# Weight sums by adding transfers for the first two quads, in a Strassen-Winograd decoder layer

## The reference

```python
x = layer_norm(ALPHA * x + merged @ w_out, ln1_g, ln1_b)
f = (jax.nn.silu(x @ w_ff_gate) * (x @ w_ff_up)) @ w_ff_down   # 1024 -> 2816 -> 1024
x = layer_norm(ALPHA * x + f, ln2_g, ln2_b)
```

## Time and profile before

| | |
|---|---|
| time, median of 3 runs | 923.67 us (923.64 to 924.33) |
| the profiled execution | 923.97 us, of which 922.0 us are the span from its first to its last instruction |
| busy, share of the span | PE 99%, weight loads 98%, DVE 83%, ACT 49%, POOL 35% |
| granted clock | 0.998 of full speed |
| moved by DMA | 98.49 MB, mean 107 GB/s |

### The profile page before, as it was taken

The page is one execution under the profiler, slowest core; times in us unless marked ns, Lnnn a source line. Parts: engine busy times, 40 slices in busy tenths (PEclk is TensorE's granted clock), DMA queues, the critical chain, the costliest instruction groups (busy, mean ns, idle before and its releaser), DMA issues.

```text
span 922.0 us, 18574 instructions
## 1 busy us (share of the span) xinstructions
PE 909.7 (99%) x7157; PEld 903.4 (98%) x7157; DVE 768.3 (83%) x1138; ACT 452.3 (49%) x783; POOL 326.5 (35%) x326
## 2 busy tenths in 40 slices
PE   9999999999999999999999999999999999999996
PEld 9999999999999999999999999999999999999995
DVE  3799999999869889877886699998878888878558
ACT  4422232325766634555553466676545666445442
POOL 4666565758300000000005451454732555421102
PEclk9999999999999999999999999999999999999999
DMA  7733332222436524342244221433333433333232
GB/s 228 197 91 92 90 101 85 75 69 79 133 111 230 198 77 125 100 125 81 75 130 124 82 64 29 124 107 93 92 106 95 118 96 92 92 108 92 85 85 97
DMA packets 169525, 98.49 MB, mean 107 GB/s; under 512 B 5306, under 2 KB 165602, under 8 KB 169457
## 3 DMA queue, kind: packets, MB, share of 16 engines
q1 hardware_dynamic: 167225, 96.66, 36.3%
q10 hardware_dynamic: 2232, 0.92, 0.4%
HBM read 89.94 MB, written 7.62 MB: 106 GB/s over the span
## 4 chain that ended last, share of the span: by engine, by line
PE 89%; DVE 6%; ACT 2%; issue 1%; POOL 1%; POOLq 0%; DVEq 0%; ACTq 0%
PE main L1582 38%; PE main L1743 33%; PE aux L1743 5%; PE main L1815 3%; PE aux L1582 3%; PE main L1996 1%; PE aux L1996 1%; PE aux L1568 1%; POOL h_f L914 1%; PE main L1618 1%; DVE aux L2606 0%; ACT merged L1305 0%; DVE merged L2619 0%; PE main L1606 0%; DVE r_tok L2896 0%
## 5 line engine op out<-in xcount | busy, mean ns | idle before, releaser
L785 POOL TENSOR_TENSOR w_lo<-raw,w_hi 128x1024 fp32r<-128x1024 f32 (+1 forms) x46 | 109.9, 2395 | 344.2 <-ACT w_hi L976 336.8
L1582 PE MATMUL main<-x_hi,w_lo 128*128 128x272 f32 x752 | 155.8, 288 | 0.0
L1582 PE MATMUL main<-x_hi,w_hi 128*128 128x272 f32 x752 | 155.6, 288 | 0.0
L1582 PE MATMUL main<-x_lo,w_hi 128*128 128x272 f32 x752 | 155.1, 288 | 0.0
L976 ACT ACTIVATE w_hi<-raw 128x1024 fp32r<-128x1024 f32 x103 | 108.5, 1057 | 70.0 <-PE main L1582 37.6
L1582 PEld LDWEIGHTS main<-x_hi,w_lo 128*128 128x128 f32 x752 | 118.2, 188 | 0.0
L1582 PEld LDWEIGHTS main<-x_lo,w_hi 128*128 128x128 f32 x752 | 118.1, 188 | 0.0
L1582 PEld LDWEIGHTS main<-x_hi,w_hi 128*128 128x128 f32 x752 | 117.4, 189 | 0.0
L2214 DVE SCALAR_TENSOR_TENSOR aux<-glu_pad,miscT,aux 128x512 f32<-128x512 f32 x112 | 75.1, 748 | 0.0
L922 POOL TENSOR_TENSOR h_lo<-h_f,h_hi 128x272 fp32r<-128x272 f32 x50 | 50.4, 1016 | 55.4 <-ACT h_hi L1410 54.6
L1582 PE MATMUL main<-y,w_hi 128*128 128x272 f32 x384 | 63.6, 287 | 0.0
(11 more groups left out here) (464 smaller groups left out, 2919.9 us busy)
## 6 DMA issues: line engine op xcount, KB each, us to landing
raw<-in_w_in SPq DMA_DIRECT2D x63, 512.0 KB, 4.2
raw<-in_w_ff_gate SPq DMA_DIRECT2D x22, 512.0 KB, 4.0
raw<-in_w_ff_up SPq DMA_DIRECT2D x22, 512.0 KB, 5.2
raw<-in_w_branch SPq DMA_DIRECT2D x32, 256.0 KB, 4.0
raw<-in_w_ff_down SPq DMA_DIRECT2D x32, 256.0 KB, 4.0
raw<-in_w_out SPq DMA_DIRECT2D x8, 512.0 KB, 4.2
raw<-in_w_ff_down SPq DMA_DIRECT2D x16, 192.0 KB, 4.3
kept_sums<-g_made_hi SPq DMA_DIRECT2D x4, 544.0 KB, 3.7
```

Of the source, the lines that this page charges most:

```text
L785: pool.tensor_tensor(w_lo[s][:, 0:n, :], raw[s][:, 0:n, :], w_hi[s][:, 0:n, :].bitcast(F32), ALU.subtract).then_inc(w_lo_ready, 1)
L1582: mm = pe.matmul(ps[:, h, :], w[s][:, k, :], x[:, h * HALF:(h + 1) * HALF], start=(first and k == 0 and j == 0), stop=(last and k == n - 1 ...
```

## The change

For steps 0 and 1 the four weight sums are no longer made by DVE. SP loads b11, b22 and b21 a second time, into `w_sum[s][0]`, `[1]` and `[2]` (256 KB each), and POOL issues four transfers that add to what is there: b12 onto the first (T1), T1 onto the second (T2), b22 onto b12 in place (T3), T2 onto the third (T4). The third of these waits with the second for the first, and the fourth waits for both. The signs change with that: all four weight sums are made with plus signs, and the sums of rows, `hid_sum`, `add_12`, `add_22` and `add_rows` change theirs, with as many instructions as before. From step 2 on DVE makes the sums as before, with `add` for `subtract`. The high and low parts of step 0's sums are made later than before: `sum_high(0, 0)` after the affine step of half 1, `sum_high(0, 2)` after `x_sum_high(2)`, `sum_low(0, 0)` just ahead of `sum_low(0, 1)`.

```diff
+        Z_ADDED = (16, 48, 64)
+        def t_sum(s, j):
+            return w_sum[s][j][:, :, :] if s < 2 else sum_bank(s, j)
...
# SP, at step s
-                    sp.wait_ge(t4_ready, quads(s - 2))
+                    if s >= 4:
+                        sp.wait_ge(t4_ready, quads(s - 2) - 2)
...
+                    if s < 2:
+                        if s == 0:
+                            sp.wait_ge(unit_done, U_FF)
+                        else:
+                            sp.wait_ge(z_made[0], Z_ADDED[0])
+                        for j, (w, k0) in enumerate(((w_g, 0), (w_u, KH), (w_g, KH))):
+                            sp.dma_start(w_sum[s][j][:, :, :], w[:, k0:k0 + KH, f * P:f * P + P])\
+                              .then_inc(z_begun, 16)
# POOL
+            def add_up(s, j):
+                if j == 0:
+                    pool.wait_ge(raw_landed[2 * s + 1], landed_right(s))
+                    pool.wait_ge(z_begun, 48 * s + 48)
+                    term = raw[2 * s + 1][:, 0:KH, :]
+                else:
+                    pool.wait_ge(z_made[s], Z_ADDED[j - 1])
+                    term = w_sum[s][j - 1][:, :, :]
+                pool.dma_start(w_sum[s][j][:, :, :], term, accum_op=ALU.add).then_inc(z_made[s], 16)
+            def add_lower(s):
+                pool.wait_ge(z_made[s], Z_ADDED[0])
+                pool.dma_start(raw[2 * s + 1][:, 0:KH, :], raw[2 * s + 1][:, KH:KD, :], accum_op=ALU.add)\
+                    .then_inc(z_made[s], 16)
+            def z_sums(s):
+                add_up(s, 0)
+                add_up(s, 1)
+                add_lower(s)
+                add_up(s, 2)
+            z_sums(0)
             for k in range(KD // 2):
                 x1_lo(1, k)
+            z_sums(1)
...
-                a, b, op = {"s1": ("a21", "a22", ALU.add), "s2": ("s1", "a11", ALU.subtract),
-                            "s3": ("a11", "a21", ALU.subtract), "s4": ("a12", "s2", ALU.subtract)}[part]
+                a, b, op = {"s1": ("a21", "a22", ALU.subtract), "s2": ("s1", "a11", ALU.subtract),
+                            "s3": ("a11", "a21", ALU.subtract), "s4": ("a12", "s2", ALU.add)}[part]
...
# ACT, sum_high and right_high (which waits for Z_ADDED[1])
+                if s < 2:
+                    act.wait_ge(z_made[s], Z_ADDED[j])
+                else:
+                    act.wait_ge((t1_ready, t2_ready, t4_ready)[j], quads(s) - 2)
...
# DVE
-            sum_x(0, a21, a22, ALU.add)
-            two_sums(0)
+            sum_x(0, a21, a22, ALU.subtract)
             half_statistics(1)
-            third_sum(0)
-            sum_low(0, 0)
             inverse(1)
...
-                if is_quad(nxt):
+                if is_quad(nxt) and nxt >= 2:
                     two_sums(nxt)
...
-            last_sum(0)
             ve.wait_ge(x1_lo_ready, KD + KD // 2)
...
+            sum_low(0, 0)
             sum_low(0, 1)
```

More of the change, by code:

```diff
@@ L531, in build @@
         t1_ready, t2_ready, t3_ready, t4_ready = map(sem, ("t1_ready", "t2_ready", "t3_ready", "t4_ready"))
+        z_begun, z_made = sem("z_begun"), [sem(f"z_made{s}") for s in range(2)]
         t_hi_ready, t_lo_ready = sem("t_hi_ready"), sem("t_lo_ready")
@@ L947, in add_rows @@
                     pool.wait_ge(rdy, sums_to(s))
-                    pool.tensor_tensor(kept[:, :], kept[:, :], rows_of(s, where), ALU.add).then_inc(kept_added, 1)
+                    pool.tensor_tensor(kept[:, :], rows_of(s, where), kept[:, :],
+                                       ALU.subtract if where == "12" else ALU.add).then_inc(kept_added, 1)
             pool.wait_ge(p7_done, 1)
@@ L1334, in sum_high @@
                 p, n = s % 2, width(s)
-                act.wait_ge((t1_ready, t2_ready, t4_ready)[j], quads(s))
+                if s < 2:
+                    act.wait_ge(z_made[s], Z_ADDED[j])
+                else:
+                    act.wait_ge((t1_ready, t2_ready, t4_ready)[j], quads(s) - 2)
                 if s >= 2:
                     act.wait_ge((p5_done, p6_done, p4_done)[j], quads(s - 2))
-                src = sum_bank(s, j) if s else w_sum[p][j][:, 0:n, :]
+                src = t_sum(s, j)
                 act.activation(w_sum_hi[p][j][:, 0:n, :], src, ACT.Copy).then_inc(t_hi_ready, 1)
             x_sum_high(0)
-            sum_high(0, 0)
             std(1)
@@ L1362, in right_high @@
                 sl, n = 2 * (s % 2) + 1, 2 * width(s)
-                act.wait_ge(t3_ready, quads(s))
+                if s < 2:
+                    act.wait_ge(z_made[s], Z_ADDED[1])
+                else:
+                    act.wait_ge(t3_ready, quads(s) - 2)
                 if s < 2:
@@ L1474, in step @@
                     hid_high(*pair, "s4")
+            sum_high(0, 0)
             sum_high(0, 1)
-            sum_high(0, 2)
             x_sum_high(1)
@@ L1482, in _ @@
             x_sum_high(2)
+            sum_high(0, 2)
             right_high(0)
@@ L2625, in halves_of @@
                         raw[sl][:, n:2 * n, :], raw[sl + 1][:, n:2 * n, :])
-            def t_sum(s, j):
-                return sum_bank(s, j) if s else w_sum[0][j][:, 0:width(s), :]
             def two_sums(s):
@@ L2634, in two_sums @@
                 ve.wait_ge(raw_landed[2 * (s % 2) + 1], landed_right(s))
-                if s >= 2:
+                if s >= 3:
                     ve.wait_ge(t_lo_ready, 3 * quads(s) - 3)
-                ve.tensor_tensor(t_sum(s, 0), b12, b11, ALU.subtract).then_inc(t1_ready, 1)
-                ve.tensor_tensor(b12, b22, b12, ALU.subtract).then_inc(t3_ready, 1)
+                ve.tensor_tensor(t_sum(s, 0), b12, b11, ALU.add).then_inc(t1_ready, 1)
+                ve.tensor_tensor(b12, b22, b12, ALU.add).then_inc(t3_ready, 1)
             def third_sum(s):
[L2642 to L2646, removed]
-            def last_sum(s):
[L2650 to L2655, removed]
+                ve.wait_ge(t_hi_ready, 3 * quads(s) - 2)
+                ve.tensor_tensor(t_sum(s, 1), halves_of(s)[3], t_sum(s, 0), ALU.add).then_inc(t2_ready, 1)
+            def last_sum(s):
+                ve.wait_ge(t_hi_ready, 3 * quads(s) - 1)
+                ve.wait_ge(t_lo_ready, 3 * quads(s) - 2)
+                ve.tensor_tensor(t_sum(s, 2), halves_of(s)[2], t_sum(s, 1), ALU.add).then_inc(t4_ready, 1)
             def sum_low(s, j):
@@ L2660, in sum_low @@
                 ve.wait_ge(t_hi_ready, 3 * quads(s) - 2 + j)
+                if s < 2 and j < 2:
+                    ve.wait_ge(z_made[s], Z_ADDED[j + 1])
                 if s >= 2:
@@ L2726, in add_11 @@
                         ve.wait_ge(hid_1_ready, ffs(s) - 1)
+                    else:
+                        ve.wait_ge(tile_out[1], T_FF + 3)
                 else:
@@ L2739, in add_12 @@
                 out = bank_of(s, "c") if is_ff(s) else rows_of(s, "12")
-                ve.tensor_tensor(out, bank_of(s, "c"), kept_2[:, :], ALU.add).then_inc(c12_ready, 1)
+                ve.tensor_tensor(out, bank_of(s, "c"), kept_2[:, :], ALU.subtract if is_ff(s) else ALU.add)\
+                  .then_inc(c12_ready, 1)
             def add_22(s):
@@ L2751, in add_22 @@
                 out = up_2[:, :] if is_ff(s) else rows_of(s, "22")
-                ve.tensor_tensor(out, bank_of(s, "a"), kept_5[:, :], ALU.add).then_inc(c22_ready, 1)
+                ve.tensor_tensor(out, kept_5[:, :], bank_of(s, "a"), ALU.subtract).then_inc(c22_ready, 1)
             def add_21(s):
@@ L2792, in step @@
                 if is_quad(nxt):
-                    third_sum(nxt)
+                    if nxt >= 2:
+                        third_sum(nxt)
                     sum_low(nxt, 0)
@@ L2799, in step @@
                 if is_quad(nxt):
-                    last_sum(nxt)
+                    if nxt >= 2:
+                        last_sum(nxt)
                     sum_low(nxt, 1)
@@ L2824, in _ @@
             sum_x_low(0)
+            sum_low(0, 0)
             sum_low(0, 1)
             ve.wait_ge(x_sum_ready, 2)
-            sum_x(2, a12, x_sum[:, 1, :, :], ALU.subtract)
+            sum_x(2, a12, x_sum[:, 1, :, :], ALU.add)
             ff_product(0, slot(1))
```

## The result

The changed kernel took 930.81 us (median of 6 runs, 929.53 to 931.50); the kernel before, timed beside it on the same chip, 924.05 us (6 runs, 923.64 to 925.27). The ratio is 1.0066 with a 95% interval of 1.0056 to 1.0077: slower by 6.1 us by the ratio, by 6.8 us between the medians. The forecast was 922.7 us with a range to 926.2 us, so it was wrong in the time and in the sign. The profiled execution is one of 931.5 us, its span 929.7 us.

A forecast was written before the change was run, and what follows sets the result against it. PE, busy 99% of the span, was taken as the bound. Two waits gone (-1.41 us) and POOL late (+0.4 us) gave -1.0 us, so 923.0 us profiled and 922.7 us median; range 921.6 to 926.2 us.

The forecast's parts named there:

- The two old waits: PE's step 0 waits for keep_2 and add_22: both go as DVE loses four instructions, gaining 0.51 and 0.90, together 1.41 us.
- The sign changes: Add and subtract swapped one for one on DVE and POOL: costed at 0, bounds plus and minus 0.1 us.
- The second batch: Step 1's four adding transfers behind POOL's low parts, from about 565.7: no cost up to about 5.5 us per transfer.
- The limit: Feed-forward prologue: POOL must be free by 561.9 for half 1's low parts; every us later costs PE one us.
- rival 1: POOL blocked by four transfers ahead of half 1's low parts, 553 to 566: slower, up to 926.1 us or more; chance 0.25.
- POOL is free at 553.1 + 2L + 2D: Prologue: loads landing, then step 0's transfer chain, frees POOL at 562.3, 0.4 us past the time PE allows.
- L: Issue to landing of one adding transfer: taken as 3.7 us, bounds 2.4 and 5.9 us.
- D: POOL's time to issue one transfer: taken as 0.9 us, bounds 0.4 and 1.5 us.
- loads signalled: Step 0's three extra 256 KB loads in the prologue: signalled at 553.1, between 552.5 and 554.0.
- T1, issue to next issue: Step 0's first adding transfer, run alone before T2 is issued: 3.7 us.
- T2 and T3 together: Step 0's second and third transfers, T3 landing one issue time behind T2: 3.7 + 0.9 us.
- POOL held by T4's issue: Step 0's last transfer holds POOL for one issue time before the low parts: 0.9 us.

The follow-up runs named there:

- experiment 2: Changed kernel with T4 of step 0 moved behind POOL's four low parts of half 1: 922.45 us against 924.41 for the kernel before, ratio 0.9977.
- experiment 5: Changed kernel with step 0's sums back on DVE, only step 1's by transfers, behind POOL's low parts: 923.05 us against 924.29 for the kernel before.
- experiment 8: Changed kernel with all eight low parts of half 1 on DVE, none on POOL: 922.94 us against 924.29 for the kernel before, ratio 0.9985.
- experiment 1: Kernel before with the change's signs and operand orders, all sums on DVE, no adding transfer: 924.28 us against 924.41, ratio 0.9996.
- experiment 3: Changed kernel with SP's three extra step 1 loads waiting for T2 and T3 of step 0 instead of T1: 925.78 us against 924.41 before.
- experiment 6: Changed kernel with only step 0's sums by transfers; step 1's on DVE without extra loads: 927.32 us against 924.29 for the kernel before, ratio 1.0031.
- experiment 4: Changed kernel with 36 more matmuls, results overwritten, where PE waits for half 1's low parts: 927.72 us against 924.41 for the kernel before, ratio 1.0033.
- all_loads_late: Changed kernel with all of step 1's loads, tiles and extra ones, waiting for T2 and T3 of step 0: 930.69 us against 924.29 before.

## Why the prediction was wrong

**Right.** The two old waits: both gone for the reason given, with the 1.41 us (experiments 2, 5, 8, with bodies of -1.6, -1.6 and -1.4 us). The sign changes at 0 (experiment 1: interval -1.2 to +0.5 us). The second batch at 0: POOL's next work behind it, the first `hid_sum`, starts at 593.65 and waits for PE, not for transfers. The limit: POOL free by 561.9, and past it one us of waiting for one us of lateness (566.6 gave 4.7). The place and mechanism of rival 1, which had 0.25.

**Wrong: "POOL is free at 553.1 + 2L + 2D", 562.3.** It is free at 566.6, 4.3 us later. Term by term, in the time of the trace before:

| term | predicted | measured (after) | off by |
|---|---|---|---|
| loads signalled | 553.1 | 554.3 (556.08 - 1.78) | +1.2 |
| T1, issue to next issue | 3.7 | 4.3 (556.08 to 560.40) | +0.6 |
| T2 and T3 together | 3.7 + 0.9 | 7.4 (560.40 to 567.80) | +2.8 |
| POOL held by T4's issue | 0.9 | 0.56 (567.80 to 568.36) | -0.3 |

L was not the failed term: 4.3 us for T1 lies below the 5.1 us from which I had rival 1 decide. The failed step is "T3 is issued right behind T2 and lands one issue time D after it". It lands 6.85 us after its issue (560.95 to 567.80), so that the pair takes 7.4 us and not 4.6. Of the 2.8 us, 2.2 are the three loads that SP issues when T1 lands (6.85 against 4.65 in experiment 3 and 4.67 in experiment 6), and 0.6 are left when they are away: the pair then takes 5.2 us. Whether T3 needs its 4.65 us because T2 runs beside it or because of its form (within one tile), no run separates. I had named these loads under rival 1, but gave them no place in the sum, and had set against them that the engines are "idle but for these" from 556 on. That was no comfort: T2, T3 and the three loads alone gave a DMA share of 1.14 from 562 to 566.5.

```profile
562.00:566.50 4.50, 2.92 (x24) 2.69 (x22) 2.35 (x7) 4.50 (x13) 0.15 (x1) 1.00 1.14 250
```

The smaller miss is the landing of the first loads: the third is issued at 551.35 and signalled by 556.08, 4.7 us, though it moves only 256 KB; I had read 3.3 us off the 1 MB behind it. I took the rate of a stream for a landing time, where the earlier trace rows said 4.0 us.

**Missing: the clock.** "Past 561.9 every us costs PE one us" is right for the wait and wrong for the cost. A wait of 4.7 us took 2.7 us more in slow matmuls (experiment 4 takes these away alone), a cost that the sum put at nothing. With it, rival 1 at this lateness would have read 922.3 + 4.7 + 2.7 = 929.7 us, above even the 929.2 us that the sum gave with its highest L and D; the range would have had to reach there. Of the 8.1 us between the forecast and the median, POOL's lateness is 4.3 and the clock 2.7.

**What the notes gave.** By the Trainium skill's "DMA: Bandwidth & Descriptors", section "Anatomy of one DMA", 256 KB from GpSimd were an estimate of 2.6 us. No adding transfer here came near it: from issue to the next instruction that waits for them they took 3.6 to 4.6 us as T1 with no load beside, 4.2 to 4.7 us as T1 beside one pair of tiles, 4.65 to 4.8 us as T3 right behind T2, 6.8 to 7.1 us as T3 beside three loads. Keeping to the rows was right and didn't go far enough. The rule of the same page of the Trainium skill, "Issuing engines are not separate DMA queues", which spoke against the change, is borne out: SP's loads lengthen POOL's T3 by 2.2 us (experiment 3).

## What to carry to other kernels

Before moving sums onto an engine's transfers, list what is queued behind each wait that the engine gets, and when that is due; experiments 2 and 8 keep the transfers and the gain by moving a few lines: T4 behind the low parts, or the low parts to DVE. Price each landing in a chain beside whatever another queue issues on the same signal, and not from a single transfer. And price a wait of PE by its length plus the slow matmuls behind it: here 0.4 to 1.7 us cost nothing more, 2.4 to 2.9 us some 1.4 to 1.6 us more in the traces (in most executions of `loads_late` probably nothing), 4.7 us 2.7 us more.

## What the runs showed of the hardware that I had not expected

- An adding transfer of 256 KB from POOL keeps POOL for about 0.55 us, not for the 0.86 to 1.24 us that its issue lasts: T2 starts at 560.40, T3 at 560.95, and `x_lo` starts 0.56 us behind T4's issue.
- Its time from issue to the next instruction that waits for it: 3.6 to 4.6 us with no load beside it (T1 of step 1 in `all_loads_late`, 574.47 to 578.09, and T1 in `step1_only`, 565.62 to 570.21), 4.65 to 4.79 us for T3 issued 0.55 us behind T2, 6.8 to 7.1 us for T3 with three loads of 256 KB beside it. By the page of the profile of after, the medians over the whole kernel are 3.3 us for sums within `w_sum`, 4.2 us for those from `raw` and 5.4 us for T3's form.
- TensorE's granted clock fell to 0.50 in or behind waits of 2.4, 2.6, 2.9 and 4.7 us in the profiled executions, for 12 to 25 matmuls of 272 columns, and not with 1.7 us or less. With 2.4, 2.9 and 4.7 us it fell before PE had work again; with 2.6 us behind the wait (1.00 from 566.0 to 566.5, 0.73 from 566.5 to 567.5, PE starts again at 566.55), and by the mean clocks probably in three of ten runs only. Matmuls that compute nothing of use kept it at 1.00.
- Left open: PE's wait for DVE's `x_lo` at about 11 us was absent in the profiled executions of the kernel before and of `signs_only`, and between 0.2 and 2.0 us in all that have transfers from POOL (1.4 in after, 1.3 in `t4_late`, 2.0 in `step1_only`, 0.2 in `filled`). DVE waits there for the landing of a first weight tile. The wait for `sig` at 379 us is in after (0.5 us) and in `filled` (0.3 us, at 378) alone. Whether POOL's transfers have to do with either, and how they move the medians, was not tried; comparing bodies leaves them out.
